# One-core attention and convolution backbone: the first block's eight raw and gate outputs formed together in eight PSUM banks

## What is computed

```python
shift, scale, gate = split(silu(c) @ w_mod + b_mod)
hx = rms_norm(x, g_pre) * (1 + scale) + shift
cq, ckv, kr, gate = split(hx @ w_in, [384, 640, 704])       # the raw and the gate outputs
q = rms_norm(cq, g_q) @ w_uq                                 # U chunks
k, v = split(rms_norm(ckv, g_kv) @ w_ukv)                    # K and V chunks
q, k = rope_2d(q), rope_2d(kr)                               # then attention over all keys
```

## Time and profile before

| | before |
|---|---|
| median of 3 runs | 2895.99 us (2894.93 to 2896.38) |
| the profiled execution | 2900.12 us, of which the span is 2898.3 us |
| busy share of the span: TensorE, VectorE, ScalarE | 98%, 65%, 51% |
| mean granted TensorE clock | 0.993 of 2.4 GHz |
| bytes moved | 352.67 MB |

### The profile page before, as it was taken

The page is one execution under the profiler, slowest core; times in us unless marked ns, Lnnn a source line. Parts: engine busy times, 40 slices in busy tenths (PEclk is TensorE's granted clock), DMA queues, the critical chain, the costliest instruction groups (busy, mean ns, idle before and its releaser), DMA issues. The chain is left out here.

```text
span 2898.3 us, 41865 instructions
## 1 busy us (share of the span) xinstructions
PE 2825.9 (98%) x14253; PEld 2384.7 (82%) x14253; DVE 1895.0 (65%) x3032; ACT 1484.6 (51%) x3071; POOL 199.8 (7%) x167
## 2 busy tenths in 40 slices
PE   6999999999999999999999999999899999999998
PEld 4888888778888888888888888888788888888787
DVE  5756655567767677767767677653448596965865
ACT  5554646465656565656555565644432323233653
POOL 0000000011011101110111111110000000000000
PEclk9999999999999999999999999999899999999999
DMA  8577765621122213122221212245433333334753
GB/s 305 190 264 251 241 229 174 200 81 41 54 68 69 57 38 84 52 57 55 69 68 34 78 52 73 65 148 190 156 127 93 107 104 99 110 108 138 233 185 117
DMA packets 235317, 352.67 MB, mean 122 GB/s; under 512 B 76352, under 2 KB 138576, under 8 KB 233808
## 3 DMA queue, kind: packets, MB, share of 16 engines
q1 hardware_dynamic: 230480, 341.36, 37.1%
q10 hardware_dynamic: 4608, 8.39, 0.8%
HBM read 251.95 MB, written 97.73 MB: 121 GB/s over the span
## 5 line engine op out<-in xcount | busy, mean ns | idle before, releaser
L1380 ACT ACTIVATE at_pthi<-at_ps 128x512 fp32r<-128x512 f32 x576 | 328.3, 600 | 519.3 <-PE at_ps L1214 519.2
L1514 DVE TENSOR_REDUCE at_mx<-at_ps 128x1 f32<-128x512 f32 (+1 forms) x640 | 397.2, 634 | 203.1 <-PE at_ps L1201 197.7
L1550 DVE TENSOR_TENSOR at_ptlo<-at_ps,at_pthi 128x512 fp32r<-128x512 f32 x576 | 382.4, 688 | 184.4 <-ACT at_pthi L1380 182.4
L1371 ACT ACTIVATE at_prob<-at_ps,at_nmax 128x512 f32<-128x512 f32 (+1 forms) x640 | 407.6, 658 | 14.4 <-DVE at_nmax L1525 13.3
L196 PE MATMUL ci_ps<-h1hi,ci_whi 128*128 128x512 f32 x768 | 301.0, 392 | 5.5 <-DVE h1lo L2346 5.5
L1214 PE MATMUL at_ps<-ident,at_prob 128*128 128x128 f32 x2304 | 299.3, 273 | 3.4 <-DVE at_ptlo L1550 3.4
L197 PE MATMUL ci_ps<-h1lo,ci_whi 128*128 128x512 f32 x768 | 300.3, 391 | 0.0
L198 PE MATMUL ci_ps<-h1hi,ci_wlo 128*128 128x512 f32 x768 | 300.1, 391 | 0.0
L1214 PEld LDWEIGHTS at_ps<-ident,at_prob 128*128 128x128 f32 x2304 | 264.6, 141 | 26.5 <-DVE at_ptlo L1550 5.4
L1196 PE MATMUL at_ps<-at_khi,at_qhi 128*128 128x512 f32 (+1 forms) x640 | 240.0, 375 | 11.2 <-ACT at_prob L1371 8.6
L196 PE MATMUL at_ps<-at_pthi,at_vhi 128*128 128x512 f32 x576 | 250.2, 434 | 0.0
(11 more groups left out here) (277 smaller groups left out, 5629.5 us busy)
## 6 DMA issues: line engine op xcount, KB each, us to landing
fr_w<-in_w_front SPq DMA_DIRECT2D x75, 512.0 KB, 5.0
at_wmod<-in_w_mod SPq DMA_DIRECT2D x32, 512.0 KB, 3.5
ci_band<-in_bands SPq DMA_DIRECT2D x40, 320.0 KB, 3.5
cv_w<-in_cv_w_in SPq DMA_DIRECT2D x24, 512.0 KB, 4.5
fr_w<-in_w_front SPq DMA_DIRECT2D x24, 384.0 KB, 3.7
values<-fr_ob SPq DMA_DIRECT2D x36, 256.0 KB, 2.6
at_vst<-values SPq DMA_DIRECT2D x8, 1152.0 KB, 8.2
fr_w_mod<-in_w_modr SPq DMA_DIRECT2D x17, 512.0 KB, 5.7
```

The costliest lines, as they stand in the source:

```text
L1371: nc.scalar.activation(prob[:, j % 2, i, k], bank(h, j, i, c)[:, 0:k.stop - k.start], ACT.Exp, scale=SCALE, bias=nmax[:, i % 2:i % 2 + 1], ...
L1380: nc.scalar.activation(pthi[:, ring(j, n)], T[:, n % 2], ACT.Copy).then_inc(s_hi, 1)
L1514: nc.vector.tensor_reduce(mx[:, i % 2, c:c + 1], bank(h, j, i, c)[:, 0:k.stop - k.start], AXX, ALU.max).then_inc(s_mx, 1)
L1550: nc.vector.tensor_tensor(ptlo[:, ring(j, n)], T[:, n % 2], pthi[:, ring(j, n)].bitcast(F32), ALU.subtract).then_inc(s_lo, 1)
```

## The change

In block 0 the eight outputs R3 R4 R0 R1 R2 R5 G0 G1 (`FIRST`) no longer come one after the other. Eight steps S0 to S7 take their place, one for each channel tile k. In each, TensorE forms that tile's 24 matmuls, three for each of the eight outputs, into eight PSUM banks; the outputs are whole only at the end of S7. The weights are laid out anew for this (`w_first`). x of block 0 comes as columns, so transposes, row statistics and row scaling are gone. Each token's square sum is now formed in this layout: four squares of 128x1024 on ScalarE, five additions on VectorE, one fp32 column sum on TensorE, then a root and a reciprocal of 128x512. The dots go two by two, one shift and one scale tile a step. The steps that follow in block 0 are reordered, the kv sum stands behind G2 and the q sum behind G3. The other blocks keep their order.

```diff
+FIRST = ("R3", "R4", "R0", "R1", "R2", "R5", "G0", "G1")
+SLICES = tuple(f"S{k}" for k in range(KD))
+ORDERS = [SLICES + tuple("G2 G3 G4 K0 K1 V0 V1 U0 G5 U1 U2 G6 U3 U4 G7 U5".split())]
+ORDERS += [tuple("R3 R4 R5 R0 R1 R2 G0 G1 K0 G2 K1 G3 V0 G4 V1 U0 U1 U2 G5 U3 U4 G6 U5 G7".split())] * (NBLK - 2)
+ORDERS += [tuple("R3 R4 R5 R0 R1 R2 G0 C3 C4 C5 G1 G2 K0 G3 K1 V0 V1 U0 U1 G4 U2 U3 G5 U4 U5 G6 G7".split())]
+OPENING = {"rope_in": "S6", "cols": SLICES[1:] + ("G2",), "rows": SLICES[4:], "x_root": "G3", "x_store": "G4", "x_spread": "K0",
+           "scaled": ("K1", "V0", "V1", "U2", "G6", "U3", "U4", "G7"), "kv_sum": "G2", "kv_root": "G3", "kv_split": "G4",
+           "q_sum": "G3", "q_root": "G4", "q_split": "K0", "k_rope": "G3"}
...
+            for k in range(KD):
+                load_x(0, k)
+            sp.dma_start(cond[0], net.c_rows[0:1, :].to_broadcast([P, D])).then_inc(s_c[0], 16)
+            for dst, src in ((cc, net.c_cols), (net.bm, net.b_mod), (net.gpre, net.g_pre)):
+                sp.dma_start(dst[:], src).then_inc(s_small, 16)
+            for k in range(3):
+                load_mod(k)
+                load_w(k)
+            for k in range(3, 5):
+                load_mod(k)
             def stores(g):
...
+                if g < 3:
+                    load_mod(g + 5)
+                if g == 3:
+                    load_rows(1, 0)
...
+                if name in at["rows"][:-1]:
+                    load_rows(t + 1, at["rows"].index(name) + 1)
...
+            def block_sum():
+                pe.wait_ge(s_xsum, 1)
+                nc.tensor.matmul(SUM[:, 0], net.ones[:], t2[:], start=True, stop=True).then_inc(s_xroot, 1)
+
+            def first_slice(k, ws):
+
+                w = lambda side, o: side[:, ws, o * P:(o + 1) * P]
+                outputs = range(len(FIRST))
+                pe.wait_ge(s_whi, k + 1)
+                pe.wait_ge(s_hhi, k + 1)
                 if k == 0:
+                    pe.wait_ge(s_xinv, 1)
+                for o in outputs:
+                    nc.tensor.matmul(ps[:, o], w(whi, o), h0hi[:, k], start=k == 0, stop=False)
+                pe.wait_ge(s_wlo, k + 1)
+                if k < KD - 1:
+                    for o in outputs:
+                        nc.tensor.matmul(ps[:, o], w(wlo, o), h0hi[:, k], start=False, stop=False)
+                    pe.wait_ge(s_hlo, k + 1)
+                    for o in outputs:
+                        mm = nc.tensor.matmul(ps[:, o], w(whi, o), h0lo[:, k], start=False, stop=False)
+                    mm.then_inc(s_slice, 1)
+                    return
+                pe.wait_ge(s_hlo, k + 1)
+                for o in outputs:
+                    nc.tensor.matmul(ps[:, o], w(wlo, o), h0hi[:, k], start=False, stop=False)
+                    nc.tensor.matmul(ps[:, o], w(whi, o), h0lo[:, k], start=False, stop=True).then_inc(s_out, 1)
...
+                if g < KD:
+                    first_slice(g, ws)
+                    continue
...
-                if name == "R1":
+                if name == STEPS[t]["kv_sum"]:
                     column_sum(t, "kv")
...
+            def block_squares(r):
+                for k in (2 * r, 2 * r + 1):
+                    act.wait_ge(s_xc[k], 16)
+                nc.scalar.activation(squared[r], xc[:, 2 * r:2 * r + 2], ACT.Square).then_inc(s_xsq, 1)
...
+                if 3 <= g < KD + 2:
+                    act.wait_ge(s_slice, g - 2)
+                elif g >= 3:
                     act.wait_ge(s_out, first_out[g - 2])
...
+            for r in range(KD // 2):
+                block_squares(r)
             act.wait_ge(s_c[0], 16)
...
-            statistics()
...
+            act.wait_ge(s_xroot, 1)
+            root_mean(nc, net, rsx[:], SUM[:, 0], D).then_inc(s_xroot, 1)
...
+            hidden_high(0, 0)
+            w_high(1)
             for g, (t, name) in enumerate(seq):
+                at = STEPS[t]
+                if g < KD - 1:
+                    hidden_high(0, g + 1)
                 if g + 2 < NG:
                     w_high(g + 2)
...
+                if name in at["rows"]:
+                    squares(t + 1, at["rows"].index(name))
...
+            def block_statistics():
+
+                add = lambda out, x, y: nc.vector.tensor_tensor(out, x, y, ALU.add).then_inc(s_xadd, 1)
+                total = squared[0]
+                for r in (1, 2):
+                    dve.wait_ge(s_xsq, r + 1)
+                    if r == 2:
+                        dve.wait_ge(s_xadd, 1)
+                    add(total, total, squared[r])
+                dve.wait_ge(s_xadd, 2)
+                add(total[:, 0], total[:, 0], total[:, 1])
+                dve.wait_ge(s_xsq, KD // 2)
+                add(t2[:], squared[3][:, 0], squared[3][:, 1])
+                dve.wait_ge(s_xadd, 4)
+                nc.vector.tensor_tensor(t2[:], t2[:], total[:, 0], ALU.add).then_inc(s_xsum, 1)
+
+            def block_inverse():
+                dve.wait_ge(s_xroot, 2)
+                nc.vector.reciprocal(rsx[:], rsx[:]).then_inc(s_xinv, 1)
+                dve.wait_ge(s_xinv, 1)
...
+            def first_modulation(k):
+                for i in (k, KD + k):
+                    dve.wait_ge(s_mw[i], 16)
+                    dot(i, 0, mod_weights(i))
+                dve.wait_ge(s_mdot, 2 * k + 2)
+                modulation(0, slice(k, k + 1), k + 1)
+
+            block_statistics()
             dve.wait_ge(s_csilu, 1)
             dve.wait_ge(s_small, SMALL)
...
+            first_modulation(0)
+            block_inverse()
+            scaled(0, 0)
+            w_low(0)
+            hidden_low(0, 0)
             w_low(1)
-            dve.wait_ge(s_gains, 64)
             for g, (t, name) in enumerate(seq):
+                at = STEPS[t]
+                if g < KD - 1:
+                    first_modulation(g + 1)
+                    scaled(0, g + 1)
...
                 if g + 2 < NG:
                     w_low(g + 2)
+                if g < KD - 1:
+                    hidden_low(0, g + 1)
...
+                if name == ("G2" if t == 0 else "R0"):
                     square_sum(t, "kv")
```

More of the change, by code:

```diff
@@ L232, in front @@
     LAST = NBLK - 1
-    seq = [(t, n) for t in range(NBLK) for n in (ORDER_END if t == LAST else ORDER)]
+    seq = [(t, n) for t in range(NBLK) for n in ORDERS[t]]
     NG = len(seq)
@@ L879, in _ @@
-                if name == "R0":
+                if g < KD - 1:
+                    hidden_low(0, g + 1)
+                if name == at["x_root"]:
+                    inverse(t + 1)
+                if t == LAST - 1 and name == "U4":
+                    inverse(t + 2)
+                if t < LAST and name in at["scaled"]:
+                    scaled(t + 1, at["scaled"].index(name))
+                if after(t, name, at["scaled"]):
+                    k = at["scaled"].index(ORDERS[t][ORDERS[t].index(name) - 1])
+                    for k in (2 * k, 2 * k + 1) if t == LAST else (k,):
+                        hidden_low(t + 1, k)
```

279 lines of the change are left out of this document (99 added, 180 removed).

## The result

The changed kernel takes **2908.37 us** (median of 8 runs, 2903.92 to 2911.55), the kernel before 2897.98 us beside it (8 runs, 2894.93 to 2901.51). The ratio is 1.0032, with a 95% interval from 1.0024 to 1.0041: slower by about 9.3 us (7.0 to 11.9). That is beyond what the prediction called no change, and 2.4 us outside its range. The profiled execution is 2908.15 us with a span of 2906.3, 8.0 more than before.

A forecast was written before the change was run, and what follows sets the result against it. TensorE's dense stream was taken as the bound: 6.3 us ahead at S7, then waits of 6.0 and 2.9 us, K1 ending at 114.5 against 110.6. So 2895.99 + 3.9 = 2900 us; 8-in-10 range 2894.5 to 2906.

The forecast's parts named there:

- the start of the opening: Chain of load, squares, adds, fp32 sum, root and reciprocal ahead of the first matmul; first `scaled` at 18.9 us.
- the fourth row load: Load of block 1's rows behind the last `scaled`, let go by the third square; 3.5 us taken to land.
- the landing of the first two column tiles: First x transfers of block 0, put at 4.4 us (between 3.9 and 5.0), ahead of ScalarE's four squares.
- between that and its double, 1.4: Opening's fp32 sum of 512 columns, taken as 1.0 us, between 0.70 for 256 columns and its double.
- The ring: VectorE and ScalarE hand over within each step S0 to S7: 7.2 us a step against TensorE's 5.44.
- a wait of 6.0: TensorE, done with G2, waits 6.0 us for the kv sum behind S7.
- a wait of 2.9: TensorE, done with G3, waits 2.9 us for the q sum.
- G4 in 5.44: Chunk G4 behind the q sum, priced at 5.44 us, the pace of a dense chunk.
- third rival: Behind S7: fourth row load in 5.4 (+1.9); second half, half clock after waits (1.7); 2903.5 us, up to 2905; chance 0.20.
- The first rival: Opening keeps TensorE's pace, 5.44 us a step, last step 10.6 us earlier: -6.7, 2889 us; chance 0.08.
- Half clock in the whole opening: TensorE at 1.2 GHz throughout the opening, steps of 10.2 us, S7 25 us later: 2922 us; chance 0.03.
- the table switch: Each ScalarE table switch costs a second load's length, at the roots and G0's SiLU: +2.9, 2903 us; chance 0.04.

The follow-up runs named there:

- Experiment 10: Changed kernel with block 0's x as four 512 KB transfers over 128 partitions with 4 KB rows, not eight of 256 KB with 2 KB rows: 2903.9 us, one run.
- Experiments 7 and 8: Changed kernel with unused matmuls ahead of the fp32 sum: 130 narrow ones, 2924.93 us, ratio 1.0098; then 32 wide ones, 2900.36 us in a single run.
- experiment 1: Changed kernel with ScalarE's weight rounding of slice g+2 ahead of the hidden rounding of slice g+1: 2894.8 us, ratio 0.9983 to the kernel before.
- Experiment 2: Changed kernel with the four squares of block 1's rows at S3 to S6 instead of S4 to S7: 2902.7 us, ratio 1.0016 to the kernel before.
- experiment 6: Changed kernel with unused matmuls on TensorE during its waits, 24 at the kv sum and 8 at the q sum: 2903.34 us, ratio 1.0020.

## Why the prediction was wrong, point by point

The mechanism was right and its sign too (+3.9 forecast, +8.5 at K1's end). What failed is the size of four terms, all in one direction: the start of the opening (+2.0), the fourth row load (+0.75), the kv sum, priced at full clock (+0.55), and G4, likewise (+1.75). In us:

| term | forecast | measured | off |
|---|---|---|---|
| first `scaled` starts | 18.9 | 20.88 | +2.0 |
| part of it: adds end | 12.4 | 13.2 | +0.8 |
| part of it: the fp32 sum | 1.0 | 2.05 | +1.05 |
| first interval and six steps | 49.7 | 49.5 | -0.2 |
| last `scaled` to the first eviction | 8.0 | 8.76 | +0.75 |
| first eviction to the kv sum | 12.1 | 12.15 | 0 |
| kv sum to the q sum | 8.8 | 9.35 | +0.55 |
| q sum to G4's end | 5.9 | 7.65 | +1.75 |
| K0 and K1 | 11.1 | 10.9 | -0.2 |
| TensorE done with K1 | 114.5 | 119.15 | +4.65 |

- *"I put the landing of the first two column tiles at 4.4 ... last end 9.7".* The first pair landed at 5.11, outside my 3.9 to 5.0. Then ScalarE was held by transfers, not by its own squares: 0.36 and 0.88 us at the third and fourth, at 300 to 344 GB/s. I had taken the landing of the first transfer and never asked when the fourth pair lands. Experiment 10 bears it out: with faster transfers the start is earlier.
- *"between that and its double, 1.4, I take 1.0".* The earlier trace rows was measured in a dense stretch. At 13 us TensorE had done nothing. The bound of 1.4 was no bound, since it left out the clock. Experiments 7 and 8 show it.
- *The ring, 7.2 us a step.* 7.16 measured, and experiment 1 shows that the weight rounding's place makes it.
- *"I take 3.5" for the fourth row load.* It was issued at 73.88 and was in at 78.07, 4.2 us, close to the median of the earlier trace rows. Experiment 2 shows that it stands on the path.
- *"a wait of 6.0", "a wait of 2.9".* 5.7 and 1.8. The second is smaller only because G3, at half clock behind the first, ended later: I had named this and left it out of the sum. It costs nothing, but I had called the half clock behind the kv wait hidden altogether, and the kv sum's own share isn't: q's halves stand behind its root, and 0.5 us passes on (experiment 6).
- *G4 in 5.44.* 6.97, with the grant at 0.50 from 102 to 104; this is the third rival's second half, given 1.7 there and worth 1.45. Its condition stood in my own rows: the earlier trace rows had TensorE at half clock behind an idle time of 1.9 us, and the forecast held two waits longer than that. But five other traces of the same program behind S7 don't have it. So a rival was the right place for it, with a chance drawn from such rows, and that the profiled execution has it is luck, here bad; without it K1's end would be +7.1.
- With the half clock (+1.7) and the median row load (+0.6) in the sum it would have been +6.2, slower by just over 0.2%.
- *The third rival* put these together, with a late start of 0.6, at 2903.5 to 2905; the start was 2.0 late. K1's end plus the median used gives 2904.5. What lies between that and 2908.4 is in part the median of before itself, which three runs put 2.0 lower than the eight beside the changed kernel; the other 2 us lie within what the runs can tell, since their difference is 7.0 to 11.9 us.
- *The first rival* (the opening at TensorE's pace) didn't happen, but experiment 1 is that case made: some 13 us faster than the changed kernel, so its price of 10.6 us for the ring was right (10.7). *Half clock in the whole opening* and the table switch didn't happen: at the first root the table load runs from 15.48 for 1.28 and the root starts at 16.78, as in the earlier trace rows. The Trainium skill (ScalarE: Activation LUTs, What ACT_TABLE_LOAD costs) has 1380 ns more a switch; the trace doesn't agree.

## What to carry to other kernels

Where three engines hand a step round, write the order of each engine's program beside it and look for work of the next step that stands behind this step's wait: here one swapped pair of lines was worth some 12 us, more than the whole change. A wait taken away at one consumer shows up at the next in the same chain until other work covers the whole latency; follow it to the end before giving it a price. Take durations of TensorE's work behind a pause from rows that stood behind a pause. And before a gain of a microsecond or two is put down to an edit, lay beside it the same stretch of other traces whose program there is the same: here 1.45 us came and went with no edit at all.
